# Gated delta rule of a second transformer block: row factors and inverse steps as 128-wide matmuls, key dots shared by both directions, the context's state by transition matrices

## The chip, the cores and the metric

The kernel runs on one core of one Trainium2 chip. The metric is the device time of one launch in microseconds. TensorE (PE) multiplies; VectorE (DVE), ScalarE (ACT) and GpSimd (POOL) do element-wise work; SyncE (SP) issues most transfers. PEld in the rows is TensorE's loading of weights (the stationary operand).

## The reference

Two blocks run one after the other: four layers of a first trunk (attention and SwiGLU), then one layer of a second trunk. Everything is float32. The change lies in one part of the second trunk, the gated delta rule in chunks of 64 tokens, for 8 heads of 64 channels, in two directions, first over 256 context tokens (only the final state of each direction is used) and then over 256 latent tokens, which start from that state:

```python
def gated_delta_chunked(q, k, v, g_log, beta, s0):
    G = jnp.cumsum(gc, axis=-1)
    diff = G[..., :, None] - G[..., None, :]
    dec_strict = jnp.where(strict, jnp.exp(jnp.where(strict, diff, 0.0)), 0.0)
    dec_incl = jnp.where(incl, jnp.exp(jnp.where(incl, diff, 0.0)), 0.0)
    kk = jnp.einsum('bhnid,bhnjd->bhnij', kc, kc)
    t_mat = jnp.eye(CHUNK) + bc[..., :, None] * dec_strict * kk
    eG = jnp.exp(G)
    w_mat = triangular_solve(t_mat, (bc * eG)[..., None] * kc)
    u_v = triangular_solve(t_mat, bc[..., None] * vc)
    intra = dec_incl * jnp.einsum('bhnid,bhnjd->bhnij', qc, kc)
    q_dec = eG[..., None] * qc
    k_tail = jnp.exp(g_last[..., None] - G)[..., None] * kc

    def step(S, xs):
        u = uv_c - jnp.einsum('bhck,bhkv->bhcv', w_c, S)
        o = jnp.einsum('bhck,bhkv->bhcv', qd_c, S) + jnp.einsum('bhij,bhjv->bhiv', intra_c, u)
        S = jnp.exp(gl_c)[..., None, None] * S + jnp.einsum('bhck,bhcv->bhkv', kt_c, u)
        return S, o
```

## The kernel before

All engines run hand-written instruction streams that meet at semaphores (`then_inc`, `wait_ge`); there is no scheduler. Weights stream through a ring of four 1 MB slots (`raw`), are split by `convert` into a high part (ACT, `w_hi`, L863) and a low part (DVE, `w_lo`, L1317), and are multiplied in three passes (L1957 to L1959). `w_hi` and `w_lo` have two slots each.

The delta rule stands in the middle of the second trunk. Its tiles reuse the ring's slots, so SP holds further loads back from slot `HELD` on until the last use (`uv_done`). It runs twice over the same code: p=0 for the context, p=1 for the latents. A tile of 128 partitions holds two chunks of 64 tokens (halves `ch`), and 512 columns hold 8 heads; four such tiles, the chains c=0 to 3, cover two directions and two token tiles. In each p:

- Head. For each chain, `decay` builds log factors in a bank `A[c]`: a bf16 mask (L2351), the column part as 64x64 weights over 512 columns (L2355), and the row part as 16 matmuls of 64x64 (L2360, or L2362 for the inclusive ones). `dots` (L2374) puts k·k into `G[c]`, 16 matmuls at a time. ACT takes the exponential, DVE multiplies (L1802) and adds the identity (L1806) into `LT`. In p=1, four further inclusive decays and dots with q give `intraT`. Then PE transposes `LT` (L2406, L2410) and DVE masks the results into `XT` and `X` (L1795).
- Levels. The inverse is built in five levels. Each has, for each chain, a product with `LT` (L2421, 16 matmuls of 64x64 with 64 columns) which DVE masks into `Z`, and then a join: `X` by L2433 and `XT` by L2435, 16 matmuls each (the last level has only L2435). ACT copies `X`, DVE copies `XT`.
- Products w and u from the inverse (L2447, L2454), copied by ACT.
- The chain over four pairs of chunks: w·S (L2483), DVE subtracts (L1839), k_tail·u (L2497), DVE adds to the decayed state (L1843). In p=1 each step also writes the outputs: q_dec·S (L2490) into `A[1+d]` and intra·u (L2504) into `G[d]`, which DVE gathers in four instructions per round (L1849 to L1852).

After that come the norm and gate of the outputs (L1857 to L1868) and the next GEMMs, in order.

On the array, a 64x64 matmul uses one quarter. L2421 alternates between two quarters, L2433 and L2435 together use all four. A float32 matmul of the program is two rows in the trace (each with its own weight load), a transpose is one. So L2421 is 32 rows per chain and level, a join 64.

## Time and profile before

| | us |
|---|---|
| median of 3 runs | 2416.61 |
| lowest and highest | 2403.94 and 2421.83 |
| the profiled execution, device time | 2422.93 |
| its span in the trace | 2421.1 |
| mean granted clock | 0.906 of full |
| PE, DVE, ACT busy | 2003.0, 1406.8, 973.4 |

The profiled execution is one run and lies at the upper end of the three. The span is read from the first to the last instruction; the delta rule covers it from 1927.66 us to 2147.04 us. "PEclk" is the clock granted to TensorE, 1.00 at 2.4 GHz and 0.50 at 1.2 GHz. A row's mean duration of a matmul includes its way through the array, so the pace of a group is taken from start to start.

### The profile page before, as it was taken

Reading aid. Unit: us, or ns where it says so; the run is one execution under the profiler, and the core shown is the slowest. Engines: PE = TensorE matmul, PEld = TensorE weight load, DVE = VectorE, ACT = ScalarE, POOL = GpSimd, SP = SyncE. Lnnn points to the kernel's source line nnn. Section 1 sums busy time; section 2 is a strip of 40 time slices with the busy share of each in tenths; the row PEclk is TensorE's granted clock in tenths of the full one; section 3 lists DMA queues with packets and bytes.
Section 4 is the critical chain, followed back from the end, with each engine's and each line's share of the span. In section 5 each row is a group of like instructions: output and inputs, shape, how many; then the busy total and the mean of one; then the engine's idle time right before and its main releaser. Section 6 shows DMA issues by size and latency. Waiting matters only on the chain.

```text
span 2421.1 us, 34178 instructions
## 1 busy us (share of the span) xinstructions
PE 2003.0 (83%) x14354; PEld 1619.6 (67%) x14354; DVE 1406.8 (58%) x1435; ACT 973.4 (40%) x1414; POOL 107.5 (4%) x135
## 2 busy tenths in 40 slices
PE   3887999856899985699998978997878878767998
PEld 3666777645677763477776666776666676756787
DVE  5764777544476763367676478674325653445554
ACT  3454444433443343354345553335224411224543
POOL 1000000110000010000000000001000012000000
PEclk9998999878898996799999998898969998978999
DMA  7753888422287850168766257673112100024553
GB/s 272 259 208 106 288 305 301 149 80 77 87 285 267 305 163 24 35 223 272 235 233 210 95 177 259 233 286 126 55 52 93 47 4 3 11 82 130 169 188 105
DMA packets 215118, 393.44 MB, mean 163 GB/s; under 512 B 11305, under 2 KB 130101, under 8 KB 199605
## 3 DMA queue, kind: packets, MB, share of 16 engines
q1 hardware_dynamic: 214453, 391.12, 47.5%
q8 instruction: 114, 1.87, 0.3%
q14 instruction: 39, 0.32, 0.0%
q0 software_dynamic: 512, 0.13, 0.0%
HBM read 390.17 MB, written 1.05 MB: 162 GB/s over the span
## 4 chain that ended last, share of the span: by engine, by line
PE 58%; DVE 23%; ACT 11%; issue 6%; POOL 1%; DMA 1%; DVEq 0%; SPq 0%; ACTq 0%; POOLq 0%
PE G L1957 14%; PE G L1958 13%; PE G L1959 13%; DVE w_lo L1317 9%; ACT w_hi L863 5%; DVE acc L1361 4%; PE A L2015 2%; PE A L2421 1%; ACT z_sb L992 1%; PE A L2004 1%; PE G L2435 1%; PE A L2075 1%; PE A L2200 1%; PE A L2433 1%; POOL e_sb L748 1%
## 5 line engine op out<-in xcount | busy, mean ns | idle before, releaser
L1317 DVE TENSOR_TENSOR w_lo<-raw,w_hi 128x2048 fp32r<-128x2048 f32 (+2 forms) x265 | 571.2, 2155 | 470.5 <-ACT w_hi L863 462.7
L863 ACT CAST w_hi<-raw 128x2048 fp32r<-128x2048 f32 (+1 forms) x256 | 475.2, 1856 | 650.3 <-PE G L1959 606.1
L1957 PE MATMUL G<-w_hi,h_hi 128*128 128x512 f32 (+1 forms) x1376 | 565.3, 411 | 74.3 <-DVE w_lo L1317 27.4
L1958 PE MATMUL G<-w_lo,h_hi 128*128 128x512 f32 (+1 forms) x1376 | 550.1, 400 | 0.0
L1959 PE MATMUL G<-w_hi,h_lo 128*128 128x512 f32 (+1 forms) x1376 | 549.0, 399 | 0.0
L1957 PEld LDWEIGHTS G<-w_hi,h_hi 128*128 128x128 f32 x1376 | 274.4, 199 | 139.1 <-issue 57.9
L1959 PEld LDWEIGHTS G<-w_hi,h_lo 128*128 128x128 f32 x1376 | 271.8, 198 | 57.8
L1958 PEld LDWEIGHTS G<-w_lo,h_hi 128*128 128x128 f32 x1376 | 273.3, 199 | 53.1 <-issue 1.0
L1957 PE MATMUL G<-w_hi,act_hi 128*128 128x512 f32 (+2 forms) x704 | 284.0, 403 | 17.8 <-DVE w_lo L1317 13.0
L1361 DVE SCALAR_TENSOR_TENSOR acc<-raw,c_col,acc 128x2048 f32<-128x2048 f32 x120 | 281.9, 2349 | 24.6 <-DVE w_lo L1317 10.6
L1958 PE MATMUL G<-w_lo,act_hi 128*128 128x512 f32 (+2 forms) x704 | 279.4, 397 | 0.0
L1959 PE MATMUL G<-w_hi,act_lo 128*128 128x512 f32 (+2 forms) x704 | 278.4, 395 | 0.0
L1957 PEld LDWEIGHTS G<-w_hi,act_hi 128*128 128x128 f32 x704 | 139.9, 199 | 50.0 <-issue 16.7
L1959 PEld LDWEIGHTS G<-w_hi,act_lo 128*128 128x128 f32 x704 | 139.0, 197 | 28.5
L1958 PEld LDWEIGHTS G<-w_lo,act_hi 128*128 128x128 f32 x704 | 139.5, 198 | 27.0 <-issue 0.2
L1381 DVE TENSOR_TENSOR act_lo<-full,act_hi 128x512 fp32r<-128x512 f32 (+1 forms) x86 | 57.7, 679 | 119.3 <-ACT act_hi L890 111.2
L1975 PE MATMUL A<-consts,n_st 128*128 128x128 f32 x88 | 21.7, 393 | 65.5 <-DVE n_st L1419 65.5
L2015 PE MATMUL A<-consts,acc 128*128 128x1 f32 x320 | 45.8, 277 | 30.7 <-DVE acc L1361 27.7
L2015 PEld LDWEIGHTS A<-consts,acc 128*128 128x128 f32 x320 | 46.0, 231 | 34.7 <-DVE acc L1361 27.8
L2200 PE MATMUL A<-consts,act_st 128*128 128x128 f32 x176 | 31.1, 304 | 44.7 <-DVE act_st L1617 44.3
L760 POOL MEMSET acc<- 128x2048 f32 x15 | 27.1, 1808 | 836.0 <-PE A L2015 655.3
L1975 PEld LDWEIGHTS A<-consts,n_st 128*128 128x128 f32 x88 | 13.9, 195 | 73.2 <-issue 49.1
(356 smaller groups left out, 2089.5 us busy)
## 6 DMA issues: line engine op xcount, KB each, us to landing
raw<-in_ada_w SPq DMA_DIRECT2D x96, 1024.0 KB, 5.0
raw<-in_ffn_w_gate SPq DMA_DIRECT2D x88, 512.0 KB, 4.1
raw<-in_ffn_w_up SPq DMA_DIRECT2D x88, 512.0 KB, 5.1
raw<-in_ffn_w_down SPq DMA_DIRECT2D x40, 1024.0 KB, 5.2
raw<-in_w_mlp SPq DMA_DIRECT2D x32, 1024.0 KB, 5.7
raw<-in_w_ada SPq DMA_DIRECT2D x24, 1024.0 KB, 5.1
raw<-in_w_in SPq DMA_DIRECT2D x18, 1024.0 KB, 5.0
raw<-in_sb_w_in SPq DMA_DIRECT2D x32, 512.0 KB, 4.6
```

The lines of the kernel that those rows point to most:

```text
L748: ins = nc.gpsimd.tensor_tensor(dst[:, :, :, a:a + 32], src[:, :, :, b:b + 32], for_heads(rope_t[:, 1, t, tabs, a:a + 32], heads // (tabs. ...
L760: nc.gpsimd.memset(acc[:, b % 2], 0.0).then_inc(acc_zero, 1)
L863: nc.scalar.copy(w_hi[:, u % 2, 0:len(kts), 0:n], raw[:, slot].rearrange("p (k n) -> p k n", k=UNIT_K)[:, 0:len(kts), 0:n])\
L1317: return nc.vector.tensor_tensor(w_lo[:, u % 2, ks, 0:n], raw[:, slot].rearrange("p (k n) -> p k n", k=UNIT_K)[:, ks, 0:n], w_hi[:, u % 2, ...
L1361: nc.vector.scalar_tensor_tensor(out=acc[:, b % 2], in0=raw[:, slot], scalar=c_col[:, c:c + 1], in1=acc[:, b % 2], op0=ALU.mult, op1=ALU.a ...
L1381: nc.vector.tensor_tensor(dst_lo, full[:, f % 2, 0:n * dst_lo.shape[1]].rearrange("p (a n) -> p a n", n=n), dst_hi.bitcast(F32), ALU.subtr ...
L1957: nc.tensor.matmul(banks[t][:, 0:n], x_hi[:, kt, ts], w_hi[:, u % 2, i, 0:n], start=st, stop=False)
L1958: nc.tensor.matmul(banks[t][:, 0:n], x_hi[:, kt, ts], w_lo[:, u % 2, i, 0:n], start=False, stop=False)
L1959: ins = nc.tensor.matmul(banks[t][:, 0:n], x_lo[:, kt, ts], w_hi[:, u % 2, i, 0:n], start=False, stop=en)
L1975: ins = nc.tensor.transpose(A[t][:, c * P:c * P + P], n_st[:, t, c * P:c * P + P], ident)
L2015: ins = nc.tensor.matmul(banks[0][:, dst:dst + 1], x[:, c * P:c * P + P], ones[:, 0:1], start=True, stop=True)
L2200: ins = nc.tensor.transpose(A[p % 2][:, a * SEQ + t * P:a * SEQ + t * P + P], act_st[:, t, a * P:a * P + P], ident)
```

## The change

It touches the delta rule alone, apart from semaphores of memsets.

- `decay` makes the column part with one 128x128 matmul and the row part with one more: DVE writes `diag` (the identity scaled by the row factor, one instruction per decay, two buffers), and `same_chunk` times `diag` replaces the 16 small matmuls.
- `dots` are written per token tile `G[t]` and read by both directions, so there are two calls per phase in place of four.
- `LT` is stored with each half's block in the other half's columns and zeros beside it (POOL clears these once), so that a level's product is 8 matmuls of 128x128 weights per chain in place of 16 of 64x64. DVE needs two half-height instructions per chain for it.
- In p=0, w and u come from one matmul with 128 moving columns. From them and `k_tail`, `transition` makes for each step a matrix `MT` (the decayed identity minus k_tail·w) and a vector part `b_st`; the state then needs one product and one addition per step (`advance`, `next_state`), and the three last steps stand between decays of p=1. The sign of `beG` is flipped.
- In p=1 the two output products accumulate in one bank `A[1+d]`, and DVE gathers it in two instructions per round.
- The conversion of the weight unit that stood ahead of the delta rule on ACT and DVE stands behind it; its `w_hi` and `w_lo` slot serve as `X` and `wu`. `HELD` is one smaller.

```diff
+                ident, later, start=False, stop=False)
+                pe.wait_ge(diag_ready, i + 1)
+                return nc.tensor.matmul(bank, same_chunk, diag[:, i % 2], start=False, stop=True)
...
                         for h in range(DNH):
-                            for ch in range(2):
-                                ins = nc.tensor.matmul(A[c][half_of(1 - ch), cols_of(h)], LT[half_of(ch), c, cols_of(h)], X[half_of(ch), c, cols_of(h)],
-                                                       start=True, stop=True)
+                            ins = nc.tensor.matmul(A[c][:, cols_of(h)], LT[:, c, slot_of(h)].rearrange("p b n -> p (b n)"), X[:, c, cols_of(h)],
+                                                   start=True, stop=True)
...
+            def transition(c, bank, values):
+                q, step = c // 2, c % 2
+                for h in range(DNH):
+                    for d in range(2):
+                        cs = half_of(chunk_of(step, d))
+                        tail = k_tail[cs, q, d, HD * h:HD * h + HD]
+                        x = wu[q][cs, step, h, U_AT if values else W_AT]
+                        ins = nc.tensor.matmul(bank[half_of(d), cols_of(h)], tail if values else x, x if values else tail, start=True, stop=True)
...
+            def advance(c):
+                pe.wait_ge(mt_ready, c)
+                pe.wait_ge(S_ready, c)
+                bank = G[3 if c % 2 else 2]
+                if c == 2:
+                    pe.wait_ge(b_ready, 3)
+                for h in range(DNH):
+                    for d in range(2):
+                        ins = nc.tensor.matmul(bank[half_of(d), cols_of(h)], MT[half_of(d), c, cols_of(h)], state[half_of(d), cols_of(h)], start=True, stop=True)
+                ins.then_inc(ms_done, 1)
...
+            def next_state(c):
+                dve.wait_ge(ms_done, c)
+                if c == 1:
+                    dve.wait_ge(b_ready, 3)
+                nc.vector.tensor_tensor(state, b_st[:, c], G[3 if c % 2 else 2], ALU.add).then_inc(S_ready, 1)
```

The first place is PE at the start of the levels in p=0, a product with `LT` and the first join. Before:

```order
5764 L2421 MATMUL A<-X,LT 64x64 x64
5765 L2433 MATMUL A<-Z,XT 64x64 x2
5766 L2435 MATMUL G<-XT,Z 64x64 x2
5767 L2433 MATMUL A<-Z,XT 64x64 x2
5768 L2435 MATMUL G<-XT,Z 64x64 x2
```

Of the change:

```order
5761 L2530 MATMUL A<-consts,LT 64x64 x16
5762 L2541 MATMUL A<-X,LT 128x64 x32
5763 L2553 MATMUL A<-Z,XT 64x64 x2
5764 L2555 MATMUL G<-XT,Z 64x64 x2
5765 L2553 MATMUL A<-Z,XT 64x64 x2
5766 L2555 MATMUL G<-XT,Z 64x64 x2
```

The 64 products of four chains have become 32, each over 128 partitions; the joins stand as they did.

The second place is PE between the levels of p=0 and the decays of p=1. Before, the chain alternates two products four times:

```order
6028 L2447 MATMUL G<-XT,bek 64x64 x32
6029 L2454 MATMUL G<-bv,XT 64x64 x32
6030 L2483 MATMUL A<-state,wT 64x64 x16
6031 L2497 MATMUL A<-u_st,k_tail 64x64 x16
6032 L2483 MATMUL A<-state,wT 64x64 x16
6033 L2497 MATMUL A<-u_st,k_tail 64x64 x16
6034 L2483 MATMUL A<-state,wT 64x64 x16
6035 L2497 MATMUL A<-u_st,k_tail 64x64 x16
6036 L2483 MATMUL A<-state,wT 64x64 x16
6037 L2497 MATMUL A<-u_st,k_tail 64x64 x16
6038 L2351 MATMUL A<-masks_97,ident_b 128x512
```

Of the change, where L2474 is `transition` and L2486 is `advance`:

```order
6025 L2570 MATMUL G<-raw,XT 64x128 x32
6026 L2474 MATMUL A<-wu_153,k_tail 64x64 x32
6027 L2474 MATMUL A<-k_tail,wu_153 64x64 x16
6028 L2474 MATMUL A<-k_tail,wu_154 64x64 x16
6029 L2474 MATMUL G<-k_tail,wu_154 64x64 x16
6030 L2474 MATMUL G<-wu_154,k_tail 64x64 x32
6031 L2486 MATMUL G<-state,MT 64x64 x16
6032 L2450 MATMUL A<-masks_97,ident_b 128x512
6033 L2451 MATMUL A<-neg_G,consts 128x512
6034 L2453 MATMUL A<-diag,consts_96 128x512
6035 L2463 MATMUL G<-kT_x 64x64 x16
6036 L2486 MATMUL G<-state,MT 64x64 x16
```

Seven transitions in a row stand where eight products alternated with DVE, and the steps of the state have moved between decays.

The third place is DVE at the head of p=1, in the change. Before, the eight instructions L1802 and L1806 follow the last state directly, and the four of L1811 follow them.

```order
855 L1855 TENSOR_TENSOR diag<-pos_G,masks_97 128x512 x2
856 L1882 SCALAR_TENSOR_TENSOR X<-X,G 128x512 x2
857 L1888 TENSOR_TENSOR LT<-X,masks_97 64x8x64 x2
858 L1882 SCALAR_TENSOR_TENSOR X<-X,G 128x512
859 L1888 TENSOR_TENSOR LT<-X,masks_97 64x8x64 x2
860 L1882 SCALAR_TENSOR_TENSOR X<-X,G 128x512
861 L1888 TENSOR_TENSOR LT<-X,masks_97 64x8x64 x4
862 L1855 TENSOR_TENSOR diag<-pos_G,masks_97 128x512 x2
863 L1896 TENSOR_TENSOR intraT<-intraT,G 128x512 x4
```

The adds of the identity have become eight of half height, and `diag` instructions stand ahead of and behind the block.

## Rows read from the trace of the kernel before

**Rows 1.** The page: the span, and PE's busy time.
```profile
span 2421.1 us, 34178 instructions
PE 2003.0 (83%) x14354; PEld 1619.6 (67%) x14354; DVE 1406.8 (58%) x1435; ACT 973.4 (40%) x1414; POOL 107.5 (4%) x135
```
**Rows 2.** Windows, the delta rule by stage: window, length, busy by engine, PEclk, DMA.
```profile
1927.66:1945.05 17.39, 16.17 (x419) 12.05 (x420) 10.69 (x12) 4.13 (x5) 13.18 (x12) 1.00 0.01 3
1945.05:1998.70 53.65, 41.08 (x1795) 39.07 (x1794) 30.05 (x45) 9.38 (x16) 0.65 (x1) 1.00 0.02 4
1998.70:2006.80 8.10, 6.12 (x257) 5.82 (x256) 1.36 (x3) 4.30 (x8) 0.58 (x1) 1.00 0.02 4
2006.80:2027.59 20.79, 13.99 (x257) 12.62 (x257) 8.82 (x14) 0.00 (x0) 8.60 (x9) 0.60 0.01 2
2027.59:2055.70 28.11, 28.11 (x696) 20.13 (x696) 10.48 (x18) 4.78 (x8) 7.27 (x8) 0.93 0.01 3
2055.70:2107.95 52.25, 40.41 (x1796) 38.90 (x1794) 28.63 (x43) 9.38 (x16) 0.00 (x0) 1.00 0.02 5
2107.95:2120.03 12.08, 8.42 (x392) 7.93 (x388) 1.39 (x4) 6.58 (x13) 0.00 (x0) 1.00 0.28 89
2120.03:2147.04 27.01, 19.18 (x480) 18.52 (x480) 11.57 (x19) 6.15 (x3) 0.00 (x0) 0.81 0.33 120
```
**Rows 3.** Chain that ended last, within the levels of p=0: start, length, what.
```profile
1956.57 1.04 issue
1957.61 2.72 PE A L2421 x86
...
1963.16 1.87 issue
...
1974.44 1.89 issue
```
**Rows 4.** Windows between one such gap's end and the next.
```profile
1957.61:1961.07 3.46, 3.42 (x128) 3.28 (x127) 2.03 (x3) 0.00 (x0) 0.00 (x0) 1.00 0.02 5
1961.07:1965.03 3.96, 2.09 (x127) 1.95 (x127) 1.43 (x3) 1.17 (x2) 0.00 (x0) 1.00 0.02 4
1972.35:1976.33 3.98, 2.10 (x128) 1.96 (x128) 1.38 (x2) 1.17 (x2) 0.00 (x0) 1.00 0.02 4
```
**Rows 5.** DMA queues from 1927 to 2030 us: packets, MB, share.
```profile
q8 instruction: 21, 0.34, 1.5%
```
**Rows 6.** Timeline of PE: float32 matmuls with 128 and 64 weight columns.
```profile
1912.38 0.60 PE L2300 MATMUL A<-g_all,consts 128*128 128x32 f32 x4 [0.32 <-issue]
1912.91 1.10 PE L2305 MATMUL A<-g_all,consts 128*64 128x8 f32 x16
1923.59 1.04 PE L2318 MATMUL A<-consts,dk_x 128*128 128x128 f32 x8
```
**Rows 7.** Chain that ended last, one decay and its dots in p=0.
```profile
1930.45 0.32 PE A L2351
1930.78 1.00 PE A L2355 x4
1931.78 0.87 PE A L2360 x29
...
1932.71 0.47 PE G L2374 x30
```
**Rows 8.** Chain that ended last, the first product of the chain in p=0.
```profile
2007.02 1.16 PE A L2483 x32
```
**Rows 9.** Timeline of DVE: start, length, what, idle before and its releaser.
```profile
1929.43 2.29 DVE L1317 TENSOR_TENSOR w_lo<-raw,w_hi 128x2048 fp32r<-128x2048 f32 x1 [2.26 <-ACT w_hi L863]
1939.39 1.52 DVE L1806 TENSOR_TENSOR LT<-LT,masks 128x512 f32<-128x512 f32 x1
2036.33 0.68 DVE L1806 TENSOR_TENSOR LT<-LT,masks 128x512 f32<-128x512 f32 x1
2132.78 0.69 DVE L1852 TENSOR_TENSOR o_dn<-o_dn,G 128x512 f32<-128x512 f32 x1
2148.16 1.22 DVE L1857 TENSOR_REDUCE ss<-sq_t 128x16 f32<-128x1024 f32 x1 [1.12 <-ACT sq_t L1120]
```

More of the change, by code:

```diff
@@ L823, in _ @@
             pool.wait_ge(cb_ready, 5)
-            nc.gpsimd.memset(state, 0.0).then_inc(state_zero, 1)
+            pool.wait_ge(gemm_done, u_lat + LAT_UNITS)
+            for ch in range(2):
+                link(nc.gpsimd.memset(LT[half_of(ch), :, :, ch].rearrange("p c h n -> p (c h) n"), 0.0))
+            pool.sem_inc(anti_zero, 1)
             pool.wait_ge(raw_free, HELD)
@@ L838, in _ @@
                 if p:
-                    pool.wait_ge(su_done, 4)
+                    pool.wait_ge(b_done, 4)
+                    pool.wait_ge(mt_ready, 3)
+                else:
+                    for c in range(1, 4):
+                        nc.gpsimd.tensor_tensor(in_parity(decay_I[c - 1]), all_heads(eye), by_parity(e_last[:, c]), ALU.mult)
                 for i in range(2):
@@ L1227, in _ @@
                         nc.scalar.copy(X[:, c], A[c]).then_inc(X_ready, 1)
+                if not p:
+                    for step in range(2):
+                        act.wait_ge(wu_done, step + 1)
+                        for i in range(2):
+                            ins = nc.scalar.copy(wu[0][:, step, 4 * i:4 * i + 4].rearrange("p h w n -> p (h w n)"), A[2 * step + i])
+                        ins.then_inc(wu_act, 1)
+                    for c in range(1, 4):
+                        act.wait_ge(b_done, 2 if c == 1 else 4)
+                        nc.scalar.copy(b_st[:, c], (A[2], G[0], G[2])[c - 1]).then_inc(b_ready, 1)
+                    continue
                 for q in range(2):
-                    rd = 2 * p + q
                     bank = (A, G)[q]
-                    act.wait_ge(wT_done, rd + 1)
+                    act.wait_ge(wT_done, q + 1)
                     for ch in range(2):
@@ L1235, in _ @@
                     for step in range(2):
[L1236 removed]
+                        act.wait_ge(uv_done, 2 * q + step + 1)
                         nc.scalar.copy(u_st[:, q, step], bank[2 + step]).then_inc(uv_ready, 1)
[L1238 to L1243 removed]
+                for q in range(2):
+                    act.wait_ge(qdT_done, q + 1)
+                    for ch in range(2):
+                        ins = nc.scalar.copy(q_decT[:, q, ch], (A, G)[q][ch])
+                    ins.then_inc(qdT_ready, 1)
+            convert()
             nc.scalar.preload_act_table(ACT.Sigmoid)
@@ L1823, in _ @@
                         nc.vector.tensor_copy(XT[:, c], G[c]).then_inc(XT_ready, 1)
+                if not p:
+                    for step in range(2):
+                        dve.wait_ge(wu_done, 3 + step)
+                        for i in range(2):
+                            ins = nc.vector.tensor_copy(wu[1][:, step, 4 * i:4 * i + 4].rearrange("p h w n -> p (h w n)"), G[2 * step + i])
+                        ins.then_inc(wu_dve, 1)
+                    dve.wait_ge(b_done, 2)
+                    nc.vector.tensor_copy(state, A[0]).then_inc(S_ready, 1)
+                    dve.wait_ge(tail_ready, 2)
+                    for c in range(1, 4):
+                        dve.wait_ge(mt_done, c)
+                        nc.vector.tensor_tensor(MT[:, c], decay_I[c - 1], (A[1], A[3], G[1])[c - 1], ALU.add).then_inc(mt_ready, 1)
+                    diagonal(4)
+                    diagonal(5)
+                    continue
                 for q in range(2):
@@ new lines, in _ @@
+                    pe.wait_ge(b_ready, 3)
+                    pe.wait_ge(mt_ready, 3)
+                decay(A[0], p, 0, m_strict, 4 * p).then_inc(e_done, 1)
+                dots(kT_s, kT_s, False).then_inc(dots_half, 1)
+                if p:
+                    advance(2)
+                decay(A[1], p, 1, m_strict, 4 * p + 1).then_inc(e_done, 1)
+                pe.wait_ge(dots_half, p + 1)
+                dots(kT_s, kT_s, True).then_inc(kk_done, 1)
+                if p:
+                    advance(3)
@@ new lines, in _ @@
+                for c in (2, 3):
+                    decay(A[c], p, c, m_strict, 4 * p + c).then_inc(e_done, 1)
+                if p:
+                    for c in range(2):
+                        pe.wait_ge(E_ready, 4 + c + 1)
+                        decay(A[c], p, c, m_incl, 8 + c).then_inc(in_done, 1)
+                    pe.wait_ge(L_ready, 8)
+                    dots(kT_s, qT_x, False).then_inc(dots_half, 1)
+                    pe.wait_ge(E_ready, 8)
+                    decay(A[2], p, 2, m_incl, 10).then_inc(in_done, 1)
+                    pe.wait_ge(dots_half, 3)
+                    dots(kT_s, qT_x, True).then_inc(kk_done, 1)
+                    decay(A[3], p, 3, m_incl, 11).then_inc(in_done, 1)
+                    pe.wait_ge(S_ready, 4)
@@ L2402, in _ @@
                         pe.wait_ge(ie_ready, c + 1)
-                        pe.wait_ge(intra_ready, c + 1)
+                        pe.wait_ge(intra_ready, 4)
+                    else:
+                        pe.wait_ge(L_ready, 4)
                     pe.wait_ge(LT_ready, 4 * p + c + 1)
                     for ch in range(2):
-                        nc.tensor.matmul(G[c][half_of(1 - ch)], ident[half_of(ch), half_of(ch)], LT[half_of(ch), c], start=True, stop=True)
+                        nc.tensor.matmul(heads(G[c][half_of(1 - ch)]), ident[half_of(ch), half_of(ch)], swapped(c, ch), start=True, stop=True)
                     for h in range(DNH):
```

294 lines of the change are left out of this document (164 added, 130 removed).

## Prediction, made before the run

> **What bounds the kernel now.** I read the page first, then the windows by stage, then the chain that ended last inside the levels. The page gives a span of 2421.1 us with PE busy for 83% of it [rows 1]. All edits lie between 1927.66 and 2147.04 us, 219.4 us, in which no other work runs; so the windows are the account to change, and what a stage gains is gained whole [rows 2]. The two runs of five levels take 53.65 and 52.25 us, nearly half. In them PE is busy for 41 and 40 us only, DVE for 30 and 29. The chain shows what fills the rest: idle PE put down to "issue", 1.04, 1.87 and 1.89 us long, with no engine waited for [rows 3]. Measured from the end of one gap to the end of the next, a stretch has 127 or 128 matmuls and as many weight loads, 3.46, 3.96 and 3.98 us, whether PE was busy for 3.4 us of it or for 2.1 [rows 4]. In the same time a queue of kind "instruction" brought 21 packets of 16 KB (0.34 MB) [rows 5]. I read this as PE's instruction stream arriving in blocks of 256, at best one per 3.7 us (the mean of the three stretches is 3.8; PE executed blocks of joins in 2.1). A level before is 384 pairs, three blocks, 11.3 us: it is bound by the number of instructions, not by the array.
>
> The Trainium skill (Runtime: NRT & Kernel Launch, Instruction fetch mechanics) has the blocks of 256 instructions, but calls the cost of crossing one mostly hidden. The trace disagrees for joins: about 1.9 us shows per block. If crossings were hidden in the changed kernel, the eight gaps counted below would go and the result would be 2409.8.
>
> **The levels, after.** Joins stay: a block of 128 pairs in 1.87 us of PE (2.09 less what the first load adds), 14.7 ns per pair, so 256 pairs are 3.75 us. The product with `LT` changes from 128 pairs of 64x64 to 64 pairs of 128x128 with 64 columns. Before, 86 pairs took 2.72 us, 32 ns each, 4.1 us per level [rows 3]. The new form has no row; it is bounded by neighbours. Four pairs with 128 weight columns and 32 moving ones take 0.60 us, the last lasting some 0.27, so (0.60-0.27)/3 = 0.11 us from start to start. With 64 weight columns and 8 moving ones it is (1.10-0.20)/15 = 0.06. With 128 and 128 it is (1.04-0.27)/7 = 0.11 [rows 6]. So the pace is set by the 128 weight columns, the same for 32 and for 128 moving columns, and 64 lie between. I take 0.111: 64 x 0.111 = 7.1 us, against 4.1. Halving the instructions makes this product slower, since two quarters loaded side by side before.
>
> PE then needs 7.1 + 3.75 + 0.2 us (two changes between full and quarter array, 0.1 each, since the mask matmul of 512 columns takes 0.32 to the next start [rows 7] where 512 columns at 2.4 GHz are 0.21) = 11.05 a level. `Z` of chain 0 is ready when 3 products are still to run, `X` of chain 0 when 3 joins are, so DVE and ACT stay hidden. The stream needs 320 pairs, 2.5 blocks. A block that holds a good part of the slow product passes unseen; a block of joins alone lasts 1.87 us and leaves 1.85 open. Two blocks of joins per level hold one whole block in every alignment but the exact one: one gap per level, 1.85. So 12.9 us, four times, and a last level of 7.1 + 0.2 + 4.1 (128 pairs in two quarters at 32 ns) = 11.4: 63.0 in place of 53.65 and of 52.25. **+9.35 and +10.75.**
>
> **Head of p=0.** A decay before is 0.32 + 1.00 + 0.87 [rows 7]; after it is 0.32 and two 128x128 matmuls of 512 columns, 0.9 each (two quarters side by side took 1.00 for two): 2.1, nothing gained. Dots at 0.65 go from four to two, -1.3. PE is at the last decay after 4x2.1 + 2x0.65 = 9.7 us, ACT 0.7 later; DVE multiplies (0.6 start to start) and still has four half-height adds, 2.4 us (0.68 each by the full one's row, its length being set by columns [rows 9]), up to 1.5 more beside POOL (an add took 1.52 there), then 1.2 for the last transposes: 16.2 against 17.4. **-1.2.** The removed conversion and the new `diag` lie in DVE's idle time before the first exponential.
>
> **Tail of p=0.** Before 8.10 + 20.79 [rows 2], the chain mostly at clock 0.5 (mean 0.60). After: 1.0 for the last `XT`; w and u, four steps of 32 pairs with 128 moving columns in two quarters, 16 x 0.111 = 1.78 each, 7.1; seven transitions at 1.1 (1.16 for 32 pairs at full clock, first load included [rows 8]), 7.7; `advance(1)` 1.1; 0.4 for ACT's last copy of `b_st`. Sum 17.3. **-11.6.**
>
> **Head of p=1.** PE: four decays, two dots, two advances: 8.4 + 1.3 + 2.2 = 11.9. Only then can DVE write the tenth `diag` (it waits for the fourth decay), and the block of multiplies is queued behind it: 0.8, then four multiplies and four half adds, 4.8, until PE's `L_ready` wait at 17.5. Here the wait is new: two inclusive decays cover 4.2 of these 5.6 us. Then four half adds and `diag`, 3.0, the wide matmul 0.9, dots 0.65, the last decay 2.1, exponential and product 1.4, transposes 4.7: 30.3 against 28.1. **+2.2.**
>
> **Products and chain of p=1.** 12.08 stays. In the chain, DVE's gathering goes from four instructions to two at two places where PE or the end waits for it, 0.69 each [rows 9]: **-2.7.** The conversion moved behind puts 2.29 us on DVE where it idled for 1.12 (waiting for ACT's square) [rows 9]: **+1.15.** ACT's half (1.9) lies in its idle time in the chain; the ring's loads start at the same event as before.
>
> **Sum.** -1.2 + 9.35 - 11.6 + 2.2 + 10.75 - 2.7 + 1.15 = +8.0 us. The profiled execution is 2422.9, so it would become 2430.9; the median of the runs shown is 2416.6, so I predict 2424.6. About 1% (24 us) is what a measurement here can tell from no change.
>
> **Rivals.**
> *A, the 128-wide product is cheap.* If 64 pairs run at the 32 ns that the 64x64 ones had, the product is 2.0 us, a level is bound by 2.5 blocks, 9.3, and the last by 6.1: 43.3 per run of levels, 39.4 less in all. 8.0 - 39.4 = -31.4: 2385. For it: before, PE was bound by instruction count and not by the array. Against: 0.11 in [rows 6]. The Trainium skill (TensorE: Matmul & The Clock Gate, Back-to-back issue gap) would give it: some 60 cycles for up to 64 columns, near 25 ns. Its section LDWEIGHTS prices 128 columns at about 107 ns, and there the trace agrees. Chance 0.12.
> *B, load and stream do not overlap.* Then a pair costs 0.111 and its stream (four quarters at 14.7 ns, 0.059): +0.059 x 640 pairs = +38: 2462, slower. It decides from 0.136 us per pair on. Against: at 128 moving columns the stream would be twice as long and still 0.11 shows [rows 6]. Chance 0.07.
> *C, no gaps remain* because PE's queue runs ahead in the slow product: -14.8, net -6.8: 2409.8. For it: while the product runs slowly, the sequencer could get ahead of it by the entries of the queue and ask for the next block sooner; no row shows this. Against: the gaps of 1.87 and 1.89 us came two blocks after a slower product [rows 3]. Chance 0.15.
> *Forecast*, 0.60; the rest, 0.06, is anything else.
>
> **Numbers.** The likeliest case's own range is 2412 to 2436 (gaps 1.4 to 1.85, contention 0 to 3, run to run -13 to +5). To hold 8 in 10 it must take in C and part of A's side: 2396 to 2441. Faster by over 1% (below 2392.4): A and a little, 0.14. Slower (above 2440.8): B and a stray, 0.11. Within: 0.75.
>
> **What would show it.** Windows of the five levels at 61 to 64 us; the product with `LT` at 0.11 us per pair with PEld almost full; one "issue" gap of 1.4 to 1.9 us per level, 128 pairs after the last; the state of the context done within 18 us of its last level; clock 1.00 from w and u through the decays of p=1; a PE wait for DVE `X` ahead of the q dots. Wrong if a pair of the product takes under 0.08 or over 0.13 us, or if the chain shows gaps of another length.

## The result, and the profile after

The kernel after takes 2426.98 us (median of 19 runs, 2421.55 to 2436.37), the kernel before 2416.61 (19 runs beside them). The ratio is 1.0049, 95% interval 1.0036 to 1.0062: half a per cent slower, clear of noise, and inside the 1% that I had called "same". The prediction was 2424.6 with a range of 2396 to 2441.

The page of after (compare [rows 1]): 1280 fewer matmuls, yet a busier PE.
```profile
span 2420.0 us, 31643 instructions
PE 2019.4 (83%) x13074; PEld 1636.5 (68%) x13074; DVE 1424.8 (59%) x1446; ACT 972.9 (40%) x1414; POOL 120.5 (5%) x139
```
Windows of after by stage, columns as in [rows 2] (PE, PEld, DVE, ACT, POOL, PEclk, DMA share and GB/s). In order: head, levels and tail of the context (p=0), then head, levels, products and chain of the latent (p=1), and what lies right behind.
```profile
1918.85:1939.73 20.88, 16.42 (x228) 10.77 (x228) 19.58 (x20) 2.42 (x5) 19.73 (x15) 0.84 0.00 1
1939.73:2000.80 61.07, 57.11 (x1474) 55.82 (x1472) 29.77 (x44) 9.37 (x16) 0.00 (x0) 1.00 0.01 3
2000.80:2015.60 14.80, 13.64 (x385) 13.51 (x386) 7.99 (x11) 3.81 (x7) 6.75 (x7) 1.00 0.01 3
2015.60:2046.87 31.27, 27.11 (x377) 15.70 (x377) 21.96 (x32) 4.78 (x8) 11.63 (x10) 0.95 0.01 2
2046.87:2108.96 62.09, 56.79 (x1472) 55.64 (x1472) 28.37 (x42) 9.37 (x16) 0.00 (x0) 1.00 0.01 3
2108.96:2120.21 11.25, 8.18 (x392) 7.77 (x388) 1.39 (x4) 6.45 (x12) 0.00 (x0) 1.00 0.29 94
2120.21:2144.20 23.99, 17.68 (x480) 16.97 (x480) 8.82 (x16) 8.08 (x4) 0.00 (x0) 0.86 0.37 136
2144.20:2157.73 13.53, 1.97 (x8) 1.57 (x8) 9.64 (x16) 3.79 (x7) 0.00 (x0) 0.56 0.24 78
```
Against [rows 2]: the levels cost 7.4 and 9.8 us more, the tail of the context 14.1 less, the heads 3.5 and 3.2 more, products and chain 0.8 and 3.0 less, and the reduction behind starts 1.3 later. The sum is +7.3 us; the forecast's was +8.0. The delta rule itself began at 1918.85 us in this execution and at 1927.66 in that of before, with the same instructions ahead of it. In the twelve other traces below it starts between 1916 and 1928 us, so an offset of this size comes with the execution; whether a part of it belongs to the kernel, one trace of before can't tell. For that reason I read stages, and take totals from medians.

A part of the 14.1 us is the clock. Timeline of PE in the kernel before, the first product of each of the four steps that the transitions replace:
```profile
2007.02 1.15 PE L2483 MATMUL A<-state,wT 64*64 64x64 f32 x32 [0.90 <-ACT u_st L1237]
2010.95 1.83 PE L2483 MATMUL A<-state,wT 64*64 64x64 f32 x32 [0.86 <-DVE state L1843]
2016.40 1.97 PE L2483 MATMUL A<-state,wT 64*64 64x64 f32 x32 [0.86 <-DVE state L1843]
2021.99 1.97 PE L2483 MATMUL A<-state,wT 64*64 64x64 f32 x32 [0.86 <-DVE state L1843]
```
The first step took 3.93 us at full clock, the next three 5.45, 5.59 and 5.60 at 1.2 GHz, 4.9 us more than three steps at full clock. After ran this whole stage at full clock. So by this estimate some 9 us of the gain are the shorter chain, and some 5 us are the low clock that it no longer meets. No run undoes the transitions, so this division is read from two traces and not tested.

The chain that ended last, inside the levels of after (compare [rows 3]). One "issue" gap per level, and the wide product of four chains in one piece of 7.29 us, 64 pairs at 0.114 us. The last line is from the levels of the latent, where the four gaps were 0.99, 1.64, 1.42 and 1.25 us:
```profile
1949.69 0.79 issue
...
1952.03 7.29 PE A L2541 x64
...
1962.85 1.27 issue
...
1964.80 7.29 PE A L2541 x64
...
1974.68 0.76 issue
...
1987.80 1.09 issue
...
2069.09 1.64 issue
```
Timeline of DVE (start, length, what) at the end of the context's head: the half-height adds last 1.3 us each, eight of them 10.2 us. In the same stretch POOL is busy for 19.73 of 20.88 us.
```profile
1926.19 2.78 DVE L1888 TENSOR_TENSOR LT<-X,masks 64x512 f32<-64x512 f32 x2
1929.61 2.27 DVE L1888 TENSOR_TENSOR LT<-X,masks 64x512 f32<-64x512 f32 x2
1932.51 5.17 DVE L1888 TENSOR_TENSOR LT<-X,masks 64x512 f32<-64x512 f32 x4
```
Timeline of PE in the head of the latent, the two longest waits for VectorE (in brackets, the idle time and its releaser):
```profile
2033.07 1.03 PE L2463 MATMUL G<-qT_x,kT_x 64*64 64x64 f32 x32 [2.38 <-DVE X L1882]
...
2041.97 0.65 PE L2526 MATMUL G<-LT,consts 64*64 64x512 f32 x2 [1.61 <-DVE intraT L1896]
```

### The profile page after: what moved, and what is told of

Read it like the earlier page. It is cut to its first block, busy times and chain, and to the rows that moved or that the text cites. A ratio compares the mean times of both kernels' runs of the same rounds, so it can differ in the third digit from the quotient of the medians.

```text
span 2420.0 us, 31643 instructions
## 1 busy us (share of the span) xinstructions
PE 2019.4 (83%) x13074; PEld 1636.5 (68%) x13074; DVE 1424.8 (59%) x1446; ACT 972.9 (40%) x1414; POOL 120.5 (5%) x139
## 4 chain that ended last, share of the span: by engine, by line
PE 59%; DVE 22%; ACT 11%; issue 5%; DMA 1%; POOL 1%; DVEq 0%; SPq 0%; ACTq 0%; POOLq 0%
PE G L2055 14%; PE G L2056 13%; PE G L2057 13%; DVE w_lo L1367 9%; ACT w_hi L903 5%; DVE acc L1411 4%; PE A L2541 3%; PE A L2113 2%; ACT z_sb L1032 1%; PE A L2102 1%; PE A L2553 1%; PE A L2173 1%; PE A L2298 1%; POOL e_sb L783 1%; PE G L2555 1%
## 5 line engine op out<-in xcount | busy, mean ns | idle before, releaser
L2541 PE MATMUL A<-X,LT 128*128 128x64 f32 x640 | 73.6, 276 | 0.0
L2541 PEld LDWEIGHTS A<-X,LT 128*128 128x128 f32 x640 | 72.2, 192 | 0.7
```

Source lines behind the costliest of these rows:

```text
L2541: ins = nc.tensor.matmul(A[c][:, cols_of(h)], LT[:, c, slot_of(h)].rearrange("p b n -> p (b n)"), X[:, c, cols_of(h)], start=True, stop=True)
```

## The experiments

My theory: the wide level product costs more array time than it saves instructions; the transitions pay; the heads are held up by VectorE. The main rival: the levels grew by something else (the padded operand, moved buffers), and the wide product is cheap. All edits are to the kernel after. This table has every run, in us. A stage is measured from its first PE instruction to the next stage's, so the levels include a last gap, and the head of the latent begins with its first `advance`, 1.5 us ahead of the first decay. The figures of after differ by so much from the windows above.

| run | median | against before, 95% | head p=0 | levels p=0 | head p=1 | levels p=1 |
|---|---|---|---|---|---|---|
| after | 2426.98 | 1.0036 to 1.0062 | 20.80 | 61.81 | 32.77 | 63.17 |
| e1_narrow | 2411.46 | 0.9952 to 0.9983 | 20.57 | 54.10 | 34.27 | 54.37 |
| e2_load64 | 2398.19 (one) | | 20.77 | 48.05 | 32.80 | 47.43 |
| e3_move32 | 2451.60 (one) | | 20.79 | 75.73 | 32.71 | 77.96 |
| e4_no_xjoin | 2371.84 (one) | | 20.57 | 39.57 | 32.52 | 38.13 |
| e5_olddecay | 2426.55 | 1.0022 to 1.0060 | 20.41 | 62.24 | 29.89 | 68.23 |
| e6_pool_late | 2426.09 | 1.0023 to 1.0065 | 15.78 | 67.21 | 32.48 | 61.80 |
| e6_again | 2419.12 (one) | | 15.77 | 67.39 | 32.48 | 63.21 |
| e7_narrow_late | 2404.33 | 0.9921 to 0.9966 | 15.59 | 54.12 | 34.13 | 53.32 |
| e8_half_wide | 2490.73 | 1.0284 to 1.0328 | 21.15 | 95.29 | 33.26 | 95.21 |
| e9_best | 2399.62 | 0.9917 to 0.9945 | 15.43 | 52.01 | 28.14 | 54.11 |
| e10_best_olddecay | 2396.73 | 0.9903 to 0.9947 | 16.10 | 52.24 | 29.67 | 52.91 |
| e11_wide_dense | 2424.35 | 0.9996 to 1.0045 | 15.78 | 69.77 | 32.04 | 63.09 |

The medians of before beside them were 2417.69 (e1, e4, e5, e6), 2419.37 (e2, e3, e7, e8), 2414.91 (e6_again, e9, e10) and 2418.48 (e11).

**The level product undone.**
```diff
-ins = nc.tensor.matmul(A[c][:, cols_of(h)], LT[:, c, slot_of(h)].rearrange("p b n -> p (b n)"), X[:, c, cols_of(h)],
-                       start=True, stop=True)
+for ch in range(2):
+    ins = nc.tensor.matmul(A[c][half_of(1 - ch), cols_of(h)], swapped(c, ch, slot_of(h)), X[half_of(ch), c, cols_of(h)],
+                           start=True, stop=True)
```


> The kernel after with one part undone: the level product goes back to 16 matmuls of 64x64 weights per chain (two chunks apart, on two quarters of the array), everything else stays. My theory: a pair with 128 weight columns is issued every 0.111 us (7.36 us of products per level in the trace of after) against 4.1 us for the 128 narrow pairs, so the two stretches of levels fall from 61.07 and 62.09 us to about the 53.65 and 52.25 us of before: together -17 us, about 2410 us in all, 0.993 of after and 0.997 of before. Rival, the levels grew for another reason than the product (padded layout of the operand, other buffers, order of the hand-offs): they stay at 61 and 62 us and the time at 2427 us. Second rival, part of the growth only (the narrow stream needs three blocks of 128 pairs per level again and pays three exposed fetches): -8 us, 2419 us.

Windows of e1_narrow, the two stretches of levels:
```profile
1946.91:2001.02 54.11, 41.19 (x1795) 39.04 (x1795) 30.30 (x46) 9.38 (x16) 0.00 (x0) 1.00 0.02 5
2048.11:2102.49 54.38, 41.02 (x1803) 39.03 (x1799) 29.21 (x44) 9.38 (x16) 0.00 (x0) 1.00 0.02 5
```
PE's busy time in them falls from 57 to 41 us and the stretches by 7.7 and 8.8 us: 16.5 of the 17 us forecast, and a median 15.5 us lower. The rest of the change, taken together, is thus a gain: e1_narrow is faster than before, by 0.2 to 0.5%. The padded operand and the moved buffers were still there, so that rival falls.

**What sets the pace of the wide product.** Two runs change one size each of the 64 pairs: 64 weight columns instead of 128 (e2), 32 moved columns instead of 64 (e3).
The first line stands for e2, the others for e3, in place of the wide product:
```diff
+ins = nc.tensor.matmul(A[c][half_of(0), cols_of(h)], LT[:, c, slot_of(h), 0], X[:, c, cols_of(h)],
...
+ms = slice(cols_of(h).start, cols_of(h).start + CH // 2)
+ins = nc.tensor.matmul(A[c][:, ms], LT[:, c, slot_of(h)].rearrange("p b n -> p (b n)"), X[:, c, ms],
```


> The kernel after, but the level product loads 128 rows by 64 columns of weights instead of 128 by 128 and yields only the first 64 of its 128 output rows (part of the computation is missing). If the number of weight columns sets the pace of 0.111 us (two cycles of 2.4 GHz for each): 0.058 us per pair, 3.7 us of products per level instead of 7.36, and the level is then bound by its 2.5 blocks of the stream (9.3 to 9.9 us instead of 12.2): the stretches fall to about 48 us each, 2400 us in all. If a fixed price of a matmul on all 128 rows sets it: no change, 61 and 62 us, 2427 us.

> The kernel after, but the level product streams only 32 of each head's 64 columns (part of the computation is missing), on the same 128 by 128 weights. If the load of the weights alone sets the pace: 0.111 us per pair stays, the stretches keep 61 and 62 us, 2427 us. If the load and the streaming add up (each streamed column at 0.42 ns or more): at least 13 ns less for a pair, 0.9 us a level, the stretches lose 4 to 5 us each, 2418 us or less.

Chain that ended last in e2_load64, one level's product, and then the window of its first stretch of levels:
```profile
1956.77 3.88 PE A L2541 x64
...
1947.58:1995.63 48.05, 40.92 (x1474) 39.13 (x1472) 30.20 (x45) 9.38 (x16) 0.00 (x0) 1.00 0.02 4
```
64 pairs in 3.88 us are 0.061 each, half of the wide one's, and the stretch is the 48 us of the first theory. Windows of e3_move32: its wide product alone in the first microseconds of the levels, then all of that stretch.
```profile
1942.18:1946.90 4.72, 4.72 (x43) 4.72 (x43) 1.00 0.01 3
...
1942.18:2017.91 75.73, 74.94 (x1474) 74.09 (x1473) 30.48 (x45) 9.38 (x16) 0.00 (x0) 0.73 0.01 3
```
43 pairs in 4.7 us at full clock: 0.11 us, the same as with 64 moved columns. The load of 128 weight columns is the whole price. The Trainium skill has it too (TensorE: Matmul & The Clock Gate, LDWEIGHTS: about 107 ns for 128 columns), and the trace agrees at 0.11 us. What neither theory expected is the clock: it was granted at 1.2 GHz for about half of each stretch, and the stretches grew to 76 and 78 us, where after, with the same pace per pair and full clock throughout, took 62 and 63. PE was busy for 75 of those 76 us by the records.

**What bounds the narrow levels.** One run on top of e1_narrow takes instructions away and leaves every hand-off.
```diff
-if not last:
+if not last and h == DNH - 1 and ch == 0:
     ins_x = nc.tensor.matmul(A[c][half_of(ch), hs], XT[half_of(1 - ch), c, hs], Z[half_of(1 - ch), c, hs], start=True, stop=True)
```


> As the one with the narrow level product, and besides 15 of the 16 joins that update the inverse itself are left out in levels 1 to 4 (part of the computation is missing); every copy, mask and semaphore stays. This takes 120 load and matmul pairs out of the 384 of a level but little work off the array. If the stream of instructions bounds a level (a block of 128 pairs costs at least 3.7 us): a full level falls from 10.7 us to about 7.6 to 8.3 us, the two stretches of levels lose 10 to 13 us each, about 2387 us. If the array's own time bounds it (14.7 ns for each of the pairs left out): 1.8 us per level, the stretches lose 7 us each, 2396 us. If the hand-offs to VectorE and ScalarE bound it: no change against the narrow product, 2410 us.

Chain of e1_narrow first: its shares in a stretch of the levels, and one level from product to product, 11.60 us. Then the window of e4_no_xjoin and its chain, where products start 7.14 and 7.54 us apart:
```profile
by line: PE A L2542 34.4%; issue 28.6%; PE A L2554 21.7%; PE G L2556 15.5%
...
1968.11 2.87 PE A L2542 x99
...
1979.71 2.85 PE A L2542 x97
```
```profile
by line: PE A L2542 50.8%; PE G L2556 45.7%; PE A L2554 2.9%; issue 1.0%
...
1938.21:1977.78 39.57, 37.91 (x1315) 37.06 (x1315) 30.29 (x46) 9.38 (x16) 0.00 (x0) 1.00 0.02 5
...
1946.38 3.39 PE A L2542 x117
...
1953.52 2.33 PE A L2542 x80
...
1961.06 3.56 PE A L2542 x118
```
The array's work hardly shrank: the joins that are left use half of the array. A product of 3.5 us leaves them 3.6 us of a level, where all 256 pairs had 3.75. PE is busy for 37.9 us against 41.2. Yet the stretches lose 14.5 and 16.2 us; what went is the "issue" time, 28.6% of the chain in e1_narrow and 1.0% here. Four full levels with 120 pairs fewer are 3.75 blocks of 128 pairs; 14.5 and 16.2 us over these are 3.9 and 4.3 us a block, more than the 10 to 13 us that I had expected. DVE's and ACT's work is the same in both. So the instruction stream bounds the narrow levels, as I had read from [rows 4], and the hand-offs don't. The pace of the stream is not one number, though: here 264 pairs passed in 7.14 us, 3.5 us per 128. The total of e4 lies 43.0 us below the profiled execution of e1_narrow (2414.85); 30.8 are in the two stretches, and 8.7 come from an earlier start of the delta rule.

**Half wide, half narrow.**
```diff
+if h % 2:
+    for ch in range(2):
+        ins = nc.tensor.matmul(A[c][half_of(1 - ch), cols_of(h)], swapped(c, ch, slot_of(h)), X[half_of(ch), c, cols_of(h)],
+                               start=True, stop=True)
+else:
     nc.tensor.matmul(A[c][:, cols_of(h)], LT[:, c, slot_of(h)].rearrange("p b n -> p (b n)"), X[:, c, cols_of(h)],
```


> The kernel after with the level product of the heads 0, 2, 4, 6 in the wide form (one matmul on 128 weight columns) and of the others in the narrow form (two on 64). With the narrow form alone a level takes 10.8 us, which is 3.0 blocks of 128 pairs at 3.4 to 4.3 us: the instruction stream bounds it, and leaving 120 pairs out gave 3.7 us a level. With the wide form alone it takes 12.2 us, which is 64 pairs at 0.111 us, 256 at 0.0147 us and a gap of 1.0 to 1.6 us: the array bounds it. Theory, the two limits can be traded: half wide is 352 pairs or 2.75 blocks (9.9 to 10.2 us) and 9.4 us of array time, so a level takes about 10.0 to 10.3 us and the two stretches 51 to 52 us instead of 54: -5 us against the narrow product alone (2406 us). Rival, a full-array matmul between quarter-array ones breaks the overlap of the narrow pairs, and the product takes 3.55 + 0.058 x 64 = 7.3 us: a level 11.5 us, the stretches 57 to 58 us, +7 us against the narrow product alone (2418 us).

Chain of e8_half_wide (start, length, what), then a window with the clock:
```profile
1948.70 0.26 PE A L2543 x4
1948.96 0.36 PE A L2546 x2
1949.32 0.26 PE A L2543 x4
...
1948.62:2043.91 95.29, 94.32 (x1631) 79.61 (x1630) 30.11 (x45) 9.36 (x16) 0.00 (x0) 0.68 0.01 2
```
Both theories fall; the rival had the direction. A round of two wide and four narrow pairs takes 0.63 us at full clock, where 2 x 0.111 and 4 x 0.029 (the pace of 117 pairs in 3.39 us above) are 0.34: 0.29 us are left for two changes between the full and the quartered array. If the narrow pairs lost their overlap as well (0.061 each, as in e2, an assumption), 0.16 us are left; no run separates the two. The Trainium skill says that a change of tiling mode drains the engine (TensorEngine Tiling (Array Packing), Key Properties). By this estimate the price is 0.08 to 0.14 us each, and I had put it at 0.1, twice a level. On top, the clock was granted at half for two thirds of the stretch (0.68 in the mean). This mixture did not trade the limits of stream and array.

**The row factors undone.** The twelve calls of `diagonal` go too.
```diff
-pe.wait_ge(diag_ready, i + 1)
-return nc.tensor.matmul(bank, same_chunk, diag[:, i % 2], start=False, stop=True)
+for h in range(DNH):
+    for ch in range(2):
+        cs = half_of(ch)
+        if i < 8:
+            ins = nc.tensor.matmul(bank[cs, cols_of(h)], lnb_G[cs, d, st, h:h + 1].broadcast_to([CH, CH]), ident[cs, cs], start=False, stop=h == DNH - 1)
...
```


> The kernel after with the row factors undone: each decay matrix gets its row factor from 16 small matmuls again instead of one wide matmul on a diagonal that VectorE builds; the twelve diagonal builds go away. My theory: the wide form gained nothing, since the twelve builds (about 1.2 us each on VectorE) delay the adds and negations behind them and TensorE waits for them in the two heads: the head of the context falls from 20.8 to about 18 us, that of the latent from 31.3 to about 28 us, in all -5 us (2422 us). Rival, the wide form is a saving of TensorE time (12 decays, 16 small matmuls each at about 0.87 us against one of about 0.25 us) and the heads are bound by TensorE: they grow by 2 and 5 us, +7 us (2434 us).

**GpSimd late.**
```diff
             pool.wait_ge(raw_free, HELD)
+            pool.wait_ge(LT_ready, 4)
...
                     pool.wait_ge(wu_done, 4)
+                    pool.wait_ge(LT_ready, 8)
```


> The kernel after, but GpSimd starts its products for the context (beta-weighted keys and values, decay diagonals, tails) only when VectorE has stored the fourth of the system's operands, and those for the latent only after the eighth. My theory: VectorE's half-height adds and diagonals took about twice their time in the head of the context because GpSimd was busy beside them for 19.7 of 20.9 us (both read SBUF only), so without it the adds fall from 1.3 to 0.7 us each and the head of the context from 20.8 to about 17 us, the head of the latent by about 1 us; the late products are hidden under 61 us of levels; in all -4 to -5 us (2422 us). Rival, the adds are slow because they cover 64 partitions in an uneven layout: they keep 1.3 us and the time stays at 2427 us. Third way, GpSimd's work now slows VectorE's masks in the levels or arrives late for the products: up to +5 us.

e6's head of the context loses 5.0 us (expected some 4), e5's head of the latent 2.9 (expected 3), but e5's head of the context only 0.4 where I had expected 2.8; and neither run changed the time. Timeline of DVE in e6_pool_late, four adds of its head; its windows: head, levels, and the part of the levels at the low clock; then that part in e5_olddecay, in the levels of the latent.
```profile
1935.94 2.80 DVE L1890 TENSOR_TENSOR LT<-X,masks 64x512 f32<-64x512 f32 x4
```
```profile
1925.17:1940.95 15.78, 14.23 (x229) 8.86 (x229) 12.16 (x20) 2.39 (x4) 2.06 (x3) 1.00 0.01 3
1940.95:2008.15 67.20, 63.23 (x1474) 62.02 (x1472) 30.27 (x45) 9.37 (x16) 12.99 (x13) 0.90 0.01 3
...
1967.60:1981.30 13.70, 13.70 (x167) 13.58 (x170) 3.46 (x5) 0.58 (x1) 0.00 (x0) 0.50 0.01 1
```
```profile
2091.70:2105.40 13.70, 13.70 (x171) 13.58 (x174) 3.46 (x5) 0.59 (x1) 0.00 (x0) 0.51 0.00 1
```
In each, the levels behind the shortened head hold 13.7 us at 1.2 GHz and take 67.2 and 68.2 us instead of 61.8 and 63.2. GpSimd's work beside them is no rival for the cause: in e5 there is none, and in e7 it is there without the loss. DVE's adds, alone now, lasted 0.69 us each for 64 partitions, as long as [rows 9] has for 128. So the 1.3 us of after were GpSimd's doing. It was slowed too: its products took up to 1.49 us each beside the adds in after, and 1.04 in e6, where they start behind them. The Trainium skill has this contention for a VectorE instruction with two inputs in SBUF beside a GpSimd one that reads SBUF (SBUF — State Buffer, Who interferes with whom), and the trace agrees. The low clock in after's head, which e6's does not have, explains some 0.8 of the 5.0 us, by this estimate: the last add of after ended at 1937.7 us, the transposes of the last chain behind it take 1.3 us at full clock in e6, and the first product came at 1939.7 and not at 1939.0.

**Chance or rule?** Three runs ask whether that low clock comes back: the same kernel on another chip, the late start with the narrow product, and the wide product with both heads made dense.

> The third kernel once more (wide level product, GpSimd late), unchanged, for a second trace. In the first one the granted clock was 0.56 from 1966 to 1980 us, in the middle of the levels, and the stretch took 67.2 us instead of 61.8; with the narrow product no trace shows a low clock inside the levels. If that is a property of this kernel, a half-clock stretch of 7 to 14 us lies within the levels of the context again and they take 65 to 67 us; that would also explain why its median gained 0.9 us where its head lost 5.0. If it was chance, the levels take 61 to 62 us and the span is about 2415 us.

> The kernel after with the narrow level product (as in the first run) and GpSimd's late start (as in the third). What is to be told apart is where the late start's gain went: its profile had the head of the context 5.0 us shorter (15.78 against 20.80 us) and the levels of the context 5.4 us longer, with a granted clock of 0.56 from 1966 to 1980 us where after had 1.00, and the timed median moved by 0.9 us only. Theory A, the clock takes back what a denser TensorE gains: the head falls to about 15.8 us, a half-clock stretch of some 7 to 14 us turns up in a later stage, and the time is about that of the narrow product alone (2411 us, within 2). Theory B, the low clock in that profile was the chance of one execution: head 15.8 us, levels 54 us, all in all -5 us against the narrow product alone (2406.5 us).

> The kernel after with GpSimd's late start and the new order on VectorE in the head of the latent, but with the wide level product (and so with half-height adds). Both heads then run dense. In the traces so far, a head at a granted clock of 1.00 was followed by a stretch of 13.7 us at 0.50 within the wide levels in three cases of four (twice in the context with the late start, once in the latent with the small row factors), while after, whose head of the context ran at 0.84, had none there. Theory A, a dense head is paid back by the clock in the wide levels: heads of 15.8 and about 28.5 us, levels of the context 67 us, those of the latent 62 to 68 us, in all about 2420 us, 1.001 to 1.003 of before. Theory B, the low stretch is independent of what is around it: levels 61.8 and 63.2 us, and with 5 and 4 us won in the heads about 2417 us for the median of after's 2427 less these, or 1.000, and no 13.7 us stretch at 0.50 within the levels. In either case, if the wide product is the loss, the time stays some 16 to 21 us above the same kernel with the narrow one (2399.6 us).

Windows of e6_again, of e7_narrow_late and of e11_wide_dense, the levels of the context; for the first and the last also the low part:
```profile
1932.06:1999.45 67.39, 63.20 (x1474) 62.00 (x1473) 30.24 (x45) 9.37 (x16) 12.99 (x13) 0.90 0.01 3
...
1958.80:1972.50 13.70, 13.70 (x155) 13.58 (x157) 3.42 (x5) 0.58 (x1) 0.00 (x0) 0.50 0.01 1
```
```profile
1935.41:1989.53 54.12, 40.97 (x1795) 38.98 (x1794) 30.09 (x45) 9.36 (x16) 13.19 (x14) 1.00 0.02 4
```
```profile
1940.05:2009.82 69.77, 65.08 (x1474) 63.74 (x1472) 30.28 (x45) 9.38 (x16) 13.01 (x13) 0.88 0.01 3
...
1990.60:2007.70 17.10, 17.10 (x151) 16.98 (x152) 4.21 (x7) 0.00 (x0) 0.00 (x0) 0.51 0.00 1
```
It comes back in all three traces of a late start with the wide product, for 13.7 to 17.1 us, and not in e7. So in these traces the clock returns, with the wide product, what GpSimd's late start gains in the head, and with the narrow one the gain is kept. The medians point the same way without proving it: from after to e6 1.0049 to 1.0044, from e1_narrow to e7 0.9968 to 0.9944, where the intervals overlap. e11 came out at 1.0021, as theory A had it (1.001 to 1.003). The rule is not complete: the levels of the latent in e6_again (63.21 us) ran at full clock although their head had no low stretch either, and e9 and e10 show 3.4 us of low clock once each in narrow levels. In after, 6.8 us of low clock lay in the head of the context, where PE was waiting for VectorE for part of it:
```profile
1930.80:1937.60 6.80, 4.93 (x87) 4.57 (x91) 6.71 (x6) 0.00 (x0) 6.80 (x6) 0.50 0.00 0
```

**A version that beats both.** e9_best is e7 with the identity added at full height (the zeros beside the operand are gone, so this is possible again) and a new order on VectorE in the head of the latent. `LT` goes back to its layout of before, so GpSimd's clears go too. e10 is e9 with the small row factors.
```diff
+if p:
+    for c in range(4):
+        negate(c)
+    diagonal(10)
+    diagonal(11)
+    for c in range(4):
+        add_eye(c)
...
-for ch in range(2):
-    cs = half_of(ch)
-    ins = nc.vector.tensor_tensor(swapped(c - 1, ch), heads(X[cs, c - 1]), over_heads(eye[cs], DNH), ALU.add)
+nc.vector.tensor_tensor(heads(LT[:, c]), heads(X[:, c]), over_heads(eye, DNH), ALU.add).then_inc(LT_ready, 1)
```


> The candidate for a version that beats both: the narrow level product and GpSimd's late start (2404.3 us together, 0.9944 of before), with two changes on VectorE. As the narrow product needs no zeros beside the operands, the identity is added at full height again, 8 adds of 0.68 us instead of 16 half-height ones of 0.68 us. And in the head of the latent the order is: four negations, the last two diagonals, the four adds, so that TensorE no longer waits behind eight adds for the tenth diagonal. The head of the context should fall from 15.6 to about 14 us, that of the latent from 34.1 to about 29.5 us (TensorE idle for 3.0 us before the dots of the query and some 2 us before the last diagonals, in the trace of the narrow product with late start), in all -6 us: 2398 us, 0.992 of before. Rival, the heads are bound by TensorE's own matmuls and the instruction stream, and VectorE's waits were cover: -1 to -2 us, 2403 us.

> The candidate before it, with the row factors again by 16 small matmuls instead of the diagonal and one wide matmul. The wide one is two passes of 512 columns (0.52 us each at full clock, so 1.03 us) against 0.87 us for the 16 small ones, and it needs 12 diagonals of 0.69 us on VectorE. Theory A, the wide form is no saving anywhere and its diagonals are waited for: the heads fall by another 1 and 3 us, 2394 us, 0.990 of before. Theory B, what is won in TensorE and VectorE is lost to 360 more pairs of instructions (2.8 blocks at 3.7 us, where a head has few of them to hide): the heads grow by 2 and 6 us, 2406 us, 0.995.

Windows of e9_best, the head of the latent, and of e10_best_olddecay, the same:
```profile
2004.09:2032.23 28.14, 26.22 (x419) 16.01 (x414) 17.40 (x29) 5.85 (x10) 8.21 (x9) 1.00 0.01 2
```
```profile
1999.86:2029.52 29.66, 27.62 (x661) 20.43 (x657) 12.78 (x21) 5.85 (x10) 12.28 (x13) 1.00 0.01 3
```
e9's head of the latent loses 6.0 us and PE is busy for 26 of its 28; the head of the context stays at 15.4 (forecast 14), with PE busy for 14.0 and waiting 1.4 us for the last multiply. The median falls by 4.7 us against e7, but the ratios are 0.9931 and 0.9944 with intervals that overlap; against e1_narrow (0.9968) the gain is clear.

The 6.0 us have three sources, by the timeline of PE in this head. One line each of e7, of e6_again (order and adds as in e7, and this head at full clock throughout) and of e11, which has the new order with half-height adds:
```profile
2020.82 0.69 PE L2465 MATMUL G<-qT_x,kT_x 64*64 64x64 f32 x32 [2.15 <-DVE X L1884]
```
```profile
2034.30 1.12 PE L2455 MATMUL A<-diag,consts 128*128 128x512 f32 x2 [1.56 <-DVE diag L1857]
```
```profile
2048.08 0.65 PE L2529 MATMUL G<-LT,consts 64*64 64x512 f32 x2 [3.79 <-DVE intraT L1899]
```
The new order takes away the first two waits, in e9 and in e11. In e11 the eight half-height adds then stand ahead of `intraT`, and PE waits 3.79 us for it, in e9 1.61. And e7's head held 6.8 us at 1.2 GHz (clock 0.90 in the mean), which costs it some 1.8 us between the first q dots and the transposes: 10.7 us against 8.8 in e6_again. e9's head ran at full clock. So of the 6.0 us the clock is about 1.8, and the order and the full-height adds share the other 4.2; the adds alone are 2.2 of them (3.79 against 1.61). e11's head kept 32.0 us where I had expected 28.5 for that wait and for 3.4 us at 1.2 GHz. e10 against e9: heads 0.7 and 1.5 us longer, medians 2396.73 and 2399.62 with intervals that overlap wholly. The wide row factor is worth nothing that can be measured, either way. Both are 0.5 to 1% faster than before.

## Why the prediction was right, point by point

- **The wide product**: 0.111 us per pair forecast, 0.114 measured. e2 and e3 confirm the reason, the number of weight columns. Rival A (32 ns a pair, 2385 us) and rival B (0.17 us a pair, 2462 us) fall.
- **The levels**: 63.0 forecast, 61.07 and 62.09 measured. One gap per level, as forecast, but of another length: 0.76 to 1.64 us of "issue" where I took 1.85, the length that followed two blocks of joins before. Six of the eight lie below the 1.4 us that I had named as their least, so by my own sign the account of the gaps was wrong in size. They sum to 9.2 us instead of 14.8; that the levels missed by 2.8 only is because ten products at 7.29 us instead of 7.1 took 1.9 of it back, and smaller terms the rest. Rival C (no gaps) got part of its mechanism right: the gaps were shorter. That the stream gains ground in the slow product is my reading of it, not tested.
- **Tail of the context**: 17.3 forecast, 14.80 measured. w and u took 7.2 us, as forecast. The step "seven transitions at 1.1" was mis-sized: with the `advance` behind them they took 5.7 us where I had put 7.7 + 1.1. The row of 1.16 us for a single product holds its first load and its last way through the array, which transitions in a row pay once. ACT's copies took 1.08 us where I had put 0.4. The gain, 14.1 us, carries the whole change. The low clock of before (mean 0.60) was in the 28.9 us that I started from, and its absence after was a sign that I had named; it held in this stage.
- **Head of the context**: forecast 16.2, measured 20.88, and this is the term that failed. I wrote "four half-height adds, 2.4 us, up to 1.5 more beside POOL". All eight adds ran beside GpSimd, at 1.3 us each: 10.2 us against 8 x 0.69 = 5.5, which is 4.7 us where I had put 1.5. The row with 1.52 us for such an add stood in [rows 9], and I applied it to half of them. Of the other 1.5 us of the miss, 0.9 is behind the last add, where the first product came 2.1 us later and I had put 1.2; the rest is not placed. e6, e7, e9 and e11 give 15.4 to 15.8 without GpSimd.
- **Head of the latent**: 30.3 forecast, 31.27 measured, with the new wait for DVE's `X` where I had put it (2.38 us; my numbers, 5.6 less 4.2, had 1.4). That the small row factors would do as well as the wide one ("nothing gained") is shown by e10 against e9.
- **Products, chain and behind**: 0, -2.7 and +1.15 forecast, -0.8, -3.0 and +1.3 measured.
- **The sum**: +8.0 against +7.3 in the stages. Misses of opposite sign (head of the context +4.7, tail -2.5, levels -2.8) hid each other. The mechanisms of the two large terms, levels and tail, were right; that the sum came within 0.7 us was luck. The medians differ by 10.4 us; the 3 us beyond the stages are not placed, and the start of the delta rule moves by more than that from one execution to the next.

## What to carry to other kernels

Count instructions and weight columns separately: here small float32 matmuls were bound by the instruction stream (3.5 to 4.3 us per 128 pairs), so that merging two quarter-array ones into a full-array one with 128 weight columns saved instructions and made the levels 17 us longer, and mixing both forms lost more. A change in a bundle can be a gain (the transitions) and a loss (the wide product) that cancel, and the windows by stage tell them apart before any experiment does. And the granted clock has to be looked at in a stage and behind it before a gain is put down to an edit: here it was some 5 us of the transitions' gain and 1.8 of e9's, and it took back what e6 had won.

## What the runs showed of the hardware that I had not expected

- The clock falls although PE is busy by the records: in e3_move32 (mean 0.73) and in e8_half_wide (0.68). Busy time alone does not tell which clock will be granted. What decides where the stretch of 13.7 or 17.1 us at 1.2 GHz falls is open; no kernel was tried that varies only that.
- A change between the full and the quartered array costs 0.08 to 0.14 us, an estimate from e8 (0.63 us a round, less 0.34 or 0.47 for its pairs, over two).
- A half-height VectorE add lasts as long as a full one (0.69 us for 512 columns), and 1.3 us beside GpSimd, whose own products go from 1.04 to 1.49 us.
- Joins on two quarters of the array run at about 0.028 us a pair (128 in 3.6 us), on four quarters at 0.0147: leaving out half of them saved instructions, but next to no array time.
